# One transformer-like layer on one core: the second half of the mixer, laid out in another order on four engines

## The reference

```python
h = rms_norm(x, g_mix)
proj = h @ w_in                                   # 4136 columns, cut into the parts below
y_conv = silu(layer_norm(causal_depthwise_conv(a * sigmoid(gate), 31 taps) + conv_b)) @ w_conv_out
# indexer: each query keeps its 128 best admissible keys (a mask)
p = softmax(q.k / 8 + bias[distance], kept keys)  # 8 heads, 2 key/value groups
y_attn = (p @ v) @ w_attn_out
x += (sigmoid(gc) * y_conv + sigmoid(ga) * y_attn) @ w_out
x += hier_moe(rms_norm(x, g_ffn))                 # 32 experts, 2 per row, all expert weights read
return rms_norm(x, g_final)
```

## Time and profile before

| | us |
|---|---|
| median of three timed runs | 720.33 (717.67 to 720.36) |
| profiled execution | 716.58 |
| its span | 714.8 |
| busy in the span: PE / POOL / DVE / ACT | 563.0 / 337.6 / 333.5 / 257.9 |
| from the fourth head of the first group (140.6) to the last projection (278.8) | 138.2 |
| first `w_attn_out` unit to first `w_conv_out` unit (282.1 to 326.4) | 44.3 |
| first expert weight issued | 377.2 |

### The profile page before, as it was taken

One profiled execution on the slowest core, in us unless ns is written; L12 is line 12 of the kernel. 1 busy time (PEld: TensorE's weight loads), 2 busy tenths in 40 slices (PEclk: granted clock), 3 DMA queues, 4 the chain that ended last, 5 costly groups with the idle time before them and its releaser, 6 DMA issues.

```text
span 714.8 us, 12235 instructions
## 1 busy us (share of the span) xinstructions
PE 563.0 (79%) x4275; PEld 380.0 (53%) x4276; DVE 333.5 (47%) x801; ACT 257.9 (36%) x441; POOL 337.6 (47%) x496
## 2 busy tenths in 40 slices
PE   3899999998898967897999803899989849786910
PEld 2577788775564645575788702454545424343400
DVE  4429999958788723436904282212121201121226
ACT  6344432334355552545431301333424322232312
POOL 5343344479999971224562005344545432533314
PEclk9999999999999987988999955999999988998965
DMA  9213532422102033021406798999999999999563
GB/s 283 63 60 104 192 101 76 118 59 60 31 29 60 0 118 117 2 70 49 146 1 236 265 412 316 396 409 408 365 396 408 409 407 408 404 401 392 221 232 124
DMA packets 58814, 149.21 MB, mean 209 GB/s; under 512 B 8661, under 2 KB 25045, under 8 KB 58783
## 3 DMA queue, kind: packets, MB, share of 16 engines
q1 hardware_dynamic: 53438, 139.89, 52.4%
q0 software_dynamic: 5200, 8.41, 3.2%
q10 hardware_dynamic: 144, 0.52, 0.2%
HBM read 145.37 MB, written 12.08 MB: 220 GB/s over the span
## 4 chain that ended last, share of the span: by engine, by line
PE 46%; DVE 23%; SPq 14%; DMA 6%; issue 5%; ACT 4%; POOL 2%; ACTq 0%; DVEq 0%; POOLq 0%
PE bank L674 23%; SPq L411 9%; PE bank L914 9%; PE bank L931 4%; DVE bm L1234 4%; DVE m L1233 4%; SPq L421 3%; DVE conv_buf L1225 2%; DMA gates<-in_w_e_up 2%; DVE bank L1263 2%; PE bank L891 2%; PE bank L774 2%; PE bank L746 2%; PE bank L766 1%; ACT conv_buf L1064 1%
## 5 line engine op out<-in xcount | busy, mean ns | idle before, releaser
L528 POOL TENSOR_TENSOR w_part<-region,w_part 128x1024 fp32r<-128x1024 f32 (+1 forms) x52 | 110.6, 2127 | 142.3 <-ACT w_part L965 142.3
L674 PE MATMUL bank<-h_hi,w_part 128*128 128x512 f32 (+1 forms) x528 | 170.1, 397 | 3.2 <-DVE h_lo L1183 1.7
L674 PEld LDWEIGHTS bank<-h_hi,w_part 128*128 128x128 f32 (+1 forms) x528 | 98.7, 187 | 34.1 <-issue 9.9
L914 PE MATMUL bank<-region,kT 128*32 128x256 f32 x1536 | 91.3, 391 | 18.4 <-DMA region<-in_w_e_up 13.6
L674 PE MATMUL bank<-h_lo,w_part 128*128 128x512 f32 (+1 forms) x264 | 103.4, 392 | 0.0
L1518 DVE TENSOR_TENSOR mask_b<-mask_b,bank 128x128 f32<-128x128 f32 x30 | 8.6, 288 | 186.7 <-ACT mask_b L1142 186.7
L965 ACT ACTIVATE w_part<-region 128x1024 fp32r<-128x1024 f32 (+1 forms) x52 | 48.0, 924 | 123.4 <-PE bank L674 123.4
L574 POOL TENSOR_TENSOR carrier<-mhalf 128x1 f32<-128x1 f32 x184 | 32.9, 196 | 124.5 <-ACT qT L1146 114.9
L914 PEld LDWEIGHTS bank<-region,kT 128*32 128x32 f32 x1536 | 55.2, 113 | 61.9 <-issue 38.9
L1263 DVE SCALAR_TENSOR_TENSOR bank<-glu,cv,bank 128x256 f32<-128x256 f32 x174 | 69.6, 482 | 0.0
L931 PE MATMUL bank<-region,mask_b 128*32 128x512 f32 x384 | 46.2, 598 | 12.2 <-DVE mask_b L1521 10.6
(11 more groups left out here) (252 smaller groups left out, 846.7 us busy)
## 6 DMA issues: line engine op xcount, KB each, us to landing
region<-in_w_e_down SPq DMA_DIRECT2D x22, 1024.0 KB, 16.5
region<-in_w_e_gate SPq DMA_DIRECT2D x44, 512.0 KB, 12.0
region<-in_w_e_up SPq DMA_DIRECT2D x44, 512.0 KB, 13.1
region<-in_w_in SPq DMA_DIRECT2D x16, 1024.0 KB, 6.0
gates<-in_w_e_gate SPq DMA_DIRECT2D x20, 512.0 KB
gates<-in_w_e_up SPq DMA_DIRECT2D x20, 512.0 KB
conv_buf<-in_w_e_down SPq DMA_DIRECT2D x10, 1024.0 KB, 18.4
region<-in_w_out SPq DMA_DIRECT2D x2, 2048.0 KB, 8.1
```

The source lines that it names most:

```text
L528: g.tensor_tensor(unit_part(u, 1), unit_raw(u), unit_part(u, 0).bitcast(F32), ALU.subtract)\
L674: last = mm(out_, a_parts[p], b_parts[q], start=start and x_ == 0, stop=stop and x_ == 2)
L914: last = mm(bank[0][32 * c:32 * c + 32, 0:FF], xTs[:, k, at_:at_ + 32], w_gu[slot][:, e, :, half, k, j * P:(j + 1) * P], start=(half == 0 ...
```

## The change: what it does

Nothing is computed that was not computed before. The order changes on PE, ACT, DVE and POOL, and 13 of POOL's 31 taps go to DVE. `FREE0` is 20, so 13 projections (104 contraction steps) are laid between the attention pieces, now in single steps (`fill(n)`): a few before a group's fourth head, a few after each key tile's transposes, a few after the product with v. All transposes use bank 6. ACT's loop over groups is written out, with the next group's exponentials in pairs of heads between the copies of key tiles.

```diff
-        FREE0 = 21
+        FREE0 = 20
+    POOL_TAPS = 18
@@ POOL
-                for j in range(3 * (u - FREE0 - 1), min(3 * (u - FREE0), TAPS)):
-                    if j >= 0:
-                        conv_tap(j)
-                if u == AO0 + 5:
+                if FREE0 < u < FREE0 + 10:
+                    for _ in range((2, 2, 2, 2, 2, 3, 2, 2, 1)[u - FREE0 - 1]):
+                        conv_tap(pool_taps)
+                        pool_taps += 1
+                if u == AO0 + 3:
@@ PE
+            logits(0, (0, 1, 2))
+            project(FREE0 - 1)
+            fill(2)
+            logits(0, (3,))
+            fill(14)
+            steps_at = ((6, 3, 0), (3, 3, 0), (3, 3, 0), (4, 2, 1), (3, 2, 0), (0, 3, 0), (3, 3, 6), (5, 1, 0))
             for i, (b, gr) in enumerate(attn):
                 if i + 1 < len(attn):
                     logits(i + 1, (0, 1, 2))
-                project(units_a[i])
-                pe.wait_ge(S["unit_ev"], units_a[i])
-                pe.wait_ge(S["p_ready"], i + 1)
...
+                fill(steps_at[i][0])
                 if i + 1 < len(attn):
                     logits(i + 1, (3,))
-                if units_b[i]:
-                    project(units_b[i])
+                for s in range(b + 1):
+                    transpose_probs(i, s)
+                    fill(steps_at[i][1])
+                heads_out(i)
+                fill(steps_at[i][2])
+            fill(NPROJ * KD)
...
             pe.wait_ge(S["o_lo"], CC)
+            channel_mean()
             for u in range(AO0, CO0):
                 branch_out(u, o_part)
-                if u == AO0 + 3:
-                    channel_mean()
+                if u == AO0 + 1:
+                    channel_variance()
                 if u == AO0 + 4:
-                    channel_variance()
-                if u == AO0 + 5:
                     spread_rstd()
@@ ACT, the seventh group as an example
+            probs_T(6, 0)
+            split_hi(30)
+            unit_out(28)
+            probs_T(6, 1)
+            exps(7, (0, 1))
+            probs_T(6, 2)
+            exps(7, (2, 3))
+            probs_T(6, 3)
+            step(29)
+            gate(gB[:, 0:4, :], 21)
+            normalise(7)
+            step(30)
@@ DVE
-            taps_at = ((6, 0), (8, 5), (4, 6), (8, 7), (5, 7), (8, 8), (5, 6), (0, 0))
-            taps_end = 10
+            taps_at = ((2, 4, 2), (1, 3, 0), (4, 4, 4), (2, 4, 3), (0, 8, 1), (2, 7, 3), (3, 13, 13))
+            taps_first, taps_last = 14, 9
...
+            conv_piece(taps_first)
+            inverse_sums(0)
+            for i in range(len(attn) - 1):
+                logits_out(i + 1, (0, 1, 2))
                 conv_piece(taps_at[i][0])
-                dve.wait_ge(S["ex_done"], i + 1)
-                v.reciprocal(ri[:, i % 2, :], sm[:, i % 2, :]).then_inc(S["ri_ready"], 1)
...
+                logits_out(i + 1, (3,))
                 conv_piece(taps_at[i][1])
+                inverse_sums(i + 1)
+                conv_piece(taps_at[i][2])
                 outputs_out(i)
...
+            conv_piece(taps_last)
+            dve.wait_ge(S["conv_step"], 2 * (CC * TAPS - POOL_TAPS))
             v.memset(m8[:], 0.0).then_inc(S["conv_ready"], 1)
+            outputs_out(len(attn) - 1)
+            attn_low(0)
+            attn_low(1)
```

More of the change, by code:

```diff
@@ L723, in _ @@
             last.then_inc(S["vt_mm"], 1)
-            for group, units in ((2, (6,)), (3, (7, 8)), (4, (9,)), (5, range(10, FREE0 - 2))):
+            for group, units in ((2, (6,)), (3, (7, 8)), (4, (9,)), (5, range(10, FREE0 - 1))):
                 index_products(group)
@@ L750, in _, with fill, transpose_probs, heads_out @@
             pe.wait_ge(S["vt_ev"], 2)
-            logits(0, (0, 1, 2))
-            project(FREE0 - 2)
-            logits(0, (3,))
-            project(FREE0 - 1)
-            for i, (b, gr) in enumerate(attn):
-                if i + 1 < len(attn):
-                    logits(i + 1, (0, 1, 2))
-                project(units_a[i])
-                pe.wait_ge(S["unit_ev"], units_a[i])
-                pe.wait_ge(S["p_ready"], i + 1)
-                for s in range(b + 1):
-                    if s >= 2:
-                        pe.wait_ge(S["pt_ev"], tiles_before[i] + s - 1)
-                    to = bank[pt_bank(i, s)]
-                    for r in range(4):
-                        last = tr(to[:, r * P:(r + 1) * P], prob[i % 2][:, r, s * P:(s + 1) * P], ident[:])
-                    last.then_inc(S["pt_mm"], 1)
+            steps = [FREE0 * KD]
+            def fill(n):
+                end = min(steps[0] + n, NPROJ * KD)
+                while steps[0] < end:
+                    u, k = divmod(steps[0], KD)
+                    upto = min(KD, k + end - steps[0])
+                    k_steps(u, range(k, upto))
+                    steps[0] += upto - k
+            def transpose_probs(i, s):
+                pe.wait_ge(S["p_ready"], i + 1)
+                pe.wait_ge(S["pt_ev"], tiles_before[i] + s)
+                for r in range(4):
+                    last = tr(bank[6][:, r * P:(r + 1) * P], prob[i % 2][:, r, s * P:(s + 1) * P], ident[:])
+                last.then_inc(S["pt_mm"], 1)
+            def heads_out(i):
+                b, gr = attn[i]
                 pe.wait_ge(S["pt_ev"], tiles_before[i + 1])
@@ L1036, in _ @@
             a(vrow[:, :, :].rearrange("p b n -> p (b n)"), bank[6][:], ACT.Copy).then_inc(S["vt_ev"], 1)
-            for group, units in ((2, (6,)), (3, (7, 8)), (4, (9,)), (5, range(10, FREE0 - 1))):
+            for group, units in ((2, (6,)), (3, (7, 8)), (4, (9,)), (5, range(10, FREE0))):
                 index_relu(group)
@@ L1059, in _, with probs_T @@
                 last.then_inc(S["p_ready"], 1)
-                if i:
+            def probs_T(i, s):
+                act.wait_ge(S["pt_mm"], tiles_before[i] + s + 1)
+                if i and s == 0:
                     act.wait_ge(S["pv_mm"], i)
-                for s in range(b + 1):
-                    act.wait_ge(S["pt_mm"], tiles_before[i] + s + 1)
-                    a(pT[:, s, :, :].rearrange("p r n -> p (r n)"), bank[pt_bank(i, s)][:], ACT.Copy)\
-                        .then_inc(S["pt_ev"], 1)
@@ new lines, in gate @@
+            def gate(chunks, units):
+                act.wait_ge(S["unit_ev"], units)
+                a(chunks, chunks, ACT.Sigmoid).then_inc(S["gate_ready"], 1)
+            exps(0)
+            step(20)
+            step(21)
+            normalise(0)
+            probs_T(0, 0)
+            exps(1)
+            step(22)
+            normalise(1)
+            probs_T(1, 0)
+            exps(2)
+            normalise(2)
+            step(23)
+            probs_T(2, 0)
+            exps(3, (0, 1))
@@ new lines, in _ @@
+            probs_T(2, 1)
+            exps(3, (2, 3))
+            split_hi(26)
+            normalise(3)
+            unit_out(24)
+            probs_T(3, 0)
+            exps(4, (0, 1))
+            probs_T(3, 1)
+            exps(4, (2, 3))
+            split_hi(27)
+            normalise(4)
+            unit_out(25)
+            probs_T(4, 0)
+            exps(5, (0, 1))
+            probs_T(4, 1)
+            exps(5, (2, 3))
+            split_hi(28)
+            probs_T(4, 2)
+            unit_out(26)
@@ L1098, in _ @@
                   bias=cv[:, c, TAPS + 2:TAPS + 3]).then_inc(S["silu_ready"], 1)
-            for c in range(CC):
                 act.wait_ge(S["silu_ready"], c + 1)
@@ L1262, in conv_half @@
                 else:
[L1263 removed]
+                    ins = v.scalar_tensor_tensor(out_, shifted, cv[:, c, j:j + 1], so_far, ALU.mult, ALU.add)
                 ins.then_inc(S["conv_step"], 1)
@@ L1335, in attn_branch @@
                     .then_inc(S["branch_ev"], 1)
-            for n in range(4):
-                attn_branch(n)
+            attn_branch(0)
+            attn_branch(1)
             dve.wait_ge(S["ln_mm"], 2)
```

137 lines of the change are left out of this document (73 added, 64 removed).

## The result

The changed kernel takes 684.78 us (median of four runs, 682.79 to 684.96), the kernel before on the same chip 719.0 (four runs). The ratio is 0.952, 95% interval 0.948 to 0.956. Run again with the later experiments it took 683.66 (six runs), ratio 0.951 (0.948 to 0.955). The forecast was 685.5, and faster. The profiled execution took 684.94 and its span is 683.0, against 716.58 and 714.8 before.

What follows compares the result with a forecast made beforehand. PE was taken to bound the mixer's second half, expert-weight DMA the end. 32.6 us up to `w_conv_out` plus 2.1 behind it, less 2 for hand-overs, gave -33: 683.6 profiled, 685.5 median; range 676 to 703.

Steps and rivals of the forecast that it cites:

- Bound and path: Mixer's second half: PE is the engine to watch; its gain, 33 us, reaches the end through the expert weight stream.
- Attention and projections: PE from the first group's fourth head to the last projection: 119.0 us instead of 138.2, ending at 259.6.
- slow products: PE in attention: last group 3.0 us too long, and 1.7 lost at granted clock 0.83 from 162 to 172.
- restarts: PE's work cut into more runs: projections add 2.1 us and transposes 0.8, together 2.9.
- the two steps that moved ahead: Two contraction steps fill the 1.74 us wait at 140.06, taking 1.4 us off the later stretch.
- DVE level with PE, low parts at their lower bound: End of attention: DVE done at 259, PE at 259.6; four low parts cost 2.8 to 5.9 us, 2.8 taken.
- the walk: Group-by-group estimate of engine times in attention: PE longer in five of seven groups, DVE waiting some 8 us.
- Layer norm: From mean to `w_conv_out`: 34.2 us instead of 44.3, one slow unit of 5.0 kept; `w_conv_out` starts at 293.8.
- Taps: POOL loses 13 taps, 37 us of 117.5; buys nothing by itself, since PE didn't wait for POOL.
- the rival of a late POOL: Taps between low weight parts hold up nine units by 1.5 us each, gain 13.5 less: 699; chance 0.08.
- I carry the second half of the mixer to the end at full value.: Behind the mixer: expert weights arrive earlier one for one with the mixer's gain, so all of it counts.
- The rival with the low clock: Layer norm: clock stays down, seven units at 5.0 instead of 2.89 and mean at 7 add 18: 703; chance 0.10.

## Why the prediction was right, point by point

*Bound and path.* Right: PE set the pace of the second half of the mixer, and what it gained came through to the first expert weight, forecast near 343 and found at 339.96. The profiled execution came within 1.4 us of its forecast (684.94 for 683.6), but by errors that cancel, which is luck: the second half of the mixer gave 38.7 instead of 33, and the early fall of the clock took 1.5 and the router 5 back, which no term held.

*Attention and projections.* From the fourth head's end (142.1) to the last projection's (256.0) PE took 113.9 us for a forecast of 119.0. Idle time of 1.1 for the 2 left explains one. The rest is busy time, which I had net 1.8 down (4.7 of slow products out, 2.9 of restarts in). It fell from

```profile
140.60:278.80 138.20, 120.25 (x557) 83.23 (x556) 90.42 (x250) 63.43 (x143) 115.24 (x74) 0.95 0.15 46
```

to

```profile
142.10:256.00 113.90, 112.82 (x552) 77.53 (x550) 106.07 (x298) 67.52 (x147) 76.43 (x47) 1.00 0.19 56
```

which, with the 1.4 of the two steps that moved ahead, is 120.25 - 1.4 - 112.82 = 6.0. Slow products were about as forecast: the clock was low only in the two places that I counted, from 167 to 171 and from 263 to 273. The term with the wrong sign is the transposes, which I charged 0.8 for standing in more runs. Before, a set of four with a wait behind it shows its whole 0.60:

```profile
152.77 0.60 PE L766 MATMUL bank<-ident,region 128*128 128x128 f32 x4
```

The set at 198.25 above shows the same 0.60, but the next product starts 0.35 behind the set's own start (198.60), since it doesn't wait for the set to end. Added up from start to start, less the waits, the 80 transposes of this stretch took 12.7 us before, 1.6 of them by the low clock of the last group, and 7.6 after: 3.5 less, where I had 0.8 more. (Ends of matmuls are modelled in the trace, so the border between such a tail and the wait behind it is not sharp; their sum is.) By the same count the restarts of the projections took about 2.6 for a forecast of 2.1.

*DVE level with PE, low parts at their lower bound.* Right. The last tap ended 1.7 us before PE's last projection, and the four low parts came out at the lower end:

```profile
254.72 2.49 DVE L1398 TENSOR_TENSOR o_part<-qT,o_part 128x512 fp32r<-128x512 f32 x4
```

2.49 for a forecast of 2.8; POOL was idle from 243.9 to 258.4. The row that gave the upper end was read a little wrong: at 259.10 POOL was splitting a weight (258.55 to 260.91) and only then ran a tap. The low parts cost PE the 1.29 us ahead of the mean. DVE's waits for PE in the groups were 5.3, on logits, for the 8 that the walk gave.

*Layer norm.* From the mean to `w_conv_out` it took 34.27 us for 34.2, with the slow unit behind the variance that I had kept (36 products in 10.82, where three units at the next row's 6.02 for two take 9.0). So close a match is in part luck: that slow unit comes from the fall at 268.5, which other executions lack, and with it `w_conv_out` starts some 3 us later than without (291.45 and 288.10 in the runs with wide products). `w_conv_out` started 2.2 us before the forecast 293.8, and its first three units took 2.3 us less than in the earlier trace rows, for a forecast of 2.1, by this line of the chain of waits:

```profile
291.58 8.44 PE bank L667 x36
```

*Taps.* Right that they buy nothing by themselves; what the text did not say is that the new order needs them. With all of them on POOL three units waited 9.1 us, where the rival of a late POOL had charged nine units with 13.5 (699; measured 695.5).

*Where a step failed.* "I carry the second half of the mixer to the end at full value." This step failed: about 5 us of the gain didn't reach the end. From the first weight to the expert rows it was to take as long as before; it takes 313.6 us instead of 308.4. SP, whose loads wait for buffers of the first expert tile, issued nothing from 388.9 to 412.2, 23.3 us, where the same pause before took 18.5 (426.2 to 444.7). The DMA stretch around it shows it: 225 us at 0.98 busy and 383 GB/s, instead of 226 at 1.00 and 394. The rival with the low clock had the right cause in the wrong place: up to the mean and through most of the norm the clock held, and the fall that cost came in products of 36 columns a hundred microseconds later. The rule of the Trainium skill ("TensorE: Matmul & The Clock Gate", section "What's actually happening") that the prediction cited for it, a low clock as the default that activity releases, fits the router's rows as far as they go: 15 idle wide products held 1.00 there.

## What to carry to other kernels

When several engines take turns over short pieces, cut the long filler into steps as long as the hand-over that it hides: here the same steps in one block per group lost 25 of 35 us. Move work between engines together with the order: the taps alone gave nothing, and the order without them 12 us less. Then look far behind the change: a stretch whose code is the same can run at another clock because it now lies elsewhere in time, and a few idle wide products there may buy it back, as 15 of them did here (4 us).

## What the hardware showed unexpectedly

A tap with both inputs in SBUF waits for POOL, one with a PSUM input doesn't. While POOL split a weight (241.54 to 243.94), two half taps over PSUM ran on VectorE and then the two that read POOL's chunk from SBUF:

```profile
241.82 0.87 DVE L1351 SCALAR_TENSOR_TENSOR conv_buf<-glu,cv,bank 128x256 f32<-128x256 f32 x2
242.61 1.62 DVE L1351 SCALAR_TENSOR_TENSOR bank<-glu,cv,conv_buf 128x256 f32<-128x256 f32 x1
244.14 0.48 DVE L1351 SCALAR_TENSOR_TENSOR bank<-glu,cv,conv_buf 128x256 f32<-128x256 f32 x1
244.54 2.43 DVE L1351 SCALAR_TENSOR_TENSOR bank<-glu,cv,bank 128x256 f32<-128x256 f32 x6
```

The two over PSUM took 0.43 each beside POOL. The first over SBUF took 1.62 and ended 0.29 behind POOL's split; the second found POOL idle and took 0.48. With the taps alone POOL was idle at both, and they took 0.49 each. With the steps in one block, POOL's split began 0.1 ahead of the first (268.81 to 271.22), and that one took 2.59 and again ended 0.29 behind the split:

```profile
268.91 2.59 DVE L1351 SCALAR_TENSOR_TENSOR bank<-glu,cv,conv_buf 128x256 f32<-128x256 f32 x1
```

The Trainium skill, "SBUF — State Buffer", section "SBUF: two separate sides", has a VectorE operation with two SBUF inputs and a GpSimd operation that reads SBUF shut each other out for a whole instruction. These rows agree.

And one list of instructions shows several clock histories: the fall at 19.5, worth 1.5 us, was in both of the changed kernel's profiles and not in that of before. The two runs of one kernel with wide products up to the experts differ in it too.
